# A recurrence of a transformer block: the offset, bonus and gate of a round's outputs move from VectorE to GpSimd, and their copies stand one level later

## The reference, cut to what matters

```python
    _, y = lax.scan(step, s0, (tm(r4), tm(w4), tm(k4), tm(v4), tm(kk), tm(a4)))
    y = tm(y)
    mean = jnp.mean(y, axis=-1, keepdims=True)
    var = jnp.mean(jnp.square(y - mean), axis=-1, keepdims=True)
    yn = ((y - mean) * lax.rsqrt(var + RWKV_LN_EPS)).reshape(B, S, RWKV_WIDTH)
    yn = yn * lnx_w.astype(f32) + lnx_b.astype(f32)
    bonus = (jnp.sum(r4 * k4 * r_k.astype(f32), axis=-1, keepdims=True) * v4).reshape(B, S, RWKV_WIDTH)
    return ((yn + bonus) * g.astype(f32)).astype(p.dtype)
```

## Time and profile before

| | |
|---|---|
| median of 3 runs | 2664.47 us |
| span of the profiled execution | 2661.1 us |
| PE busy | 2627.1 us, 99% |
| DVE busy | 1938.4 us, 73% |
| ACT busy | 1381.1 us, 52% |
| POOL busy | 133.1 us, 5% |
| chain that ended last | PE 97%, DVE 2%, ACT 1% |
| recurrence and heads | about 290 to 458 us of the span |

### The profile page before, as it was taken

How to read it: one execution, slowest core, us unless ns; L and a number is a source line. 1 busy time by engine, 2 the same in 40 slices (tenths; PEclk the granted TensorE clock), 3 DMA queues, 4 the chain that set the end, 5 groups by cost and what they waited for, 6 DMA issues and landing times.

```text
span 2661.1 us, 46024 instructions
## 1 busy us (share of the span) xinstructions
PE 2627.1 (99%) x16912; PEld 2260.6 (85%) x16912; DVE 1938.4 (73%) x2963; ACT 1381.1 (52%) x2143; POOL 133.1 (5%) x146
## 2 busy tenths in 40 slices
PE   9999998999999999999999999999999999999998
PEld 8888887889888888888888888888888888888886
DVE  6677776777777877878887666578877656765675
ACT  5555565666544534535554454345455535553553
POOL 4500001301000000000000000000000000000000
PEclk9999999999999999999999999999999999999999
DMA  7555202565787888888778855677665565565554
GB/s 236 188 184 175 74 4 99 196 197 181 279 302 274 287 299 275 295 285 281 276 272 308 291 179 184 202 274 281 243 210 190 192 192 186 190 196 192 182 190 150
DMA packets 158927, 578.41 MB, mean 217 GB/s; under 512 B 18032, under 2 KB 18576, under 8 KB 157712
## 3 DMA queue, kind: packets, MB, share of 16 engines
q1 hardware_dynamic: 155792, 563.61, 62.4%
q10 hardware_dynamic: 1936, 9.44, 0.9%
q0 software_dynamic: 1008, 2.71, 0.4%
HBM read 572.81 MB, written 2.11 MB: 216 GB/s over the span
## 4 chain that ended last, share of the span: by engine, by line
PE 97%; DVE 2%; ACT 1%; issue 0%; DMA 0%; POOL 0%; DVEq 0%; ACTq 0%
PE ps L2623 35%; PE ps L2627 18%; PE ps L2702 12%; PE ps L2703 12%; PE ps L2704 12%; PE ps L1091 1%; PE ps L1737 1%; PE ps L1104 0%; PE ps L1115 0%; PE ps L1008 0%; PE ps L2686 0%; PE ps L2687 0%; PE ps L2685 0%; PE ps L2734 0%; PE ps L656 0%
## 5 line engine op out<-in xcount | busy, mean ns | idle before, releaser
L2194 DVE TENSOR_TENSOR wlo<-raw,whi 128x1024 fp32r<-128x1024 f32 x872 | 1058.9, 1230 | 523.1 <-ACT whi L1861 519.9
L1861 ACT ACTIVATE whi<-raw 128x1024 fp32r<-128x1024 f32 x872 | 904.5, 1056 | 794.7 <-PE ps L2627 387.3
L2623 PE MATMUL ps<-xn,whi 128*128 128x512 f32 x3760 | 940.9, 392 | 2.8 <-DVE xn L2273 1.4
L2623 PEld LDWEIGHTS ps<-xn,whi 128*128 128x128 f32 x3760 | 674.7, 188 | 123.3 <-issue 2.8
L2627 PEld LDWEIGHTS ps<-xn,wlo 128*128 128x128 f32 x3760 | 510.9, 191 | 37.4 <-DVE wlo L2194 0.4
L2627 PE MATMUL ps<-xn,wlo 128*128 128x256 f32 x3760 | 520.9, 282 | 0.0
L2702 PE MATMUL ps<-whi,act_in 128*128 128x512 f32 x1120 | 436.0, 389 | 0.0
L2704 PE MATMUL ps<-whi,act_in 128*128 128x512 f32 x1120 | 435.7, 389 | 0.0
L2703 PE MATMUL ps<-wlo,act_in 128*128 128x512 f32 x1120 | 435.7, 389 | 0.0
L2702 PEld LDWEIGHTS ps<-whi,act_in 128*128 128x128 f32 x1120 | 210.2, 188 | 44.6 <-DVE wlo L2194 1.0
L2704 PEld LDWEIGHTS ps<-whi,act_in 128*128 128x128 f32 x1120 | 210.2, 188 | 43.7
(11 more groups left out here) (346 smaller groups left out, 2228.7 us busy)
## 6 DMA issues: line engine op xcount, KB each, us to landing
raw<-in_stream SPq DMA_DIRECT2D x872, 512.0 KB, 4.3
adaw<-in_ada SPq DMA_DIRECT2D x96, 512.0 KB, 5.7
adaq<-in_ada SPq DMA_DIRECT2D x96, 512.0 KB, 5.3
memx<-in_memT ACTq DMA_DIRECT2D x1, 2048.0 KB, 10.7
gate_row<-gates POOLq DMA_DIRECT2D x2, 1024.0 KB, 7.5
h<-in_xT SPq DMA_DIRECT2D x3, 512.0 KB, 5.2
lwa<-in_lora ACTq DMA_DIRECT2D x2, 512.0 KB, 4.6
lwa<-in_lora ACTq DMA_DIRECT2D x1, 1024.0 KB, 6.3
```

Of the source, the lines that this page charges most:

```text
L1861: act.activation(whi[:, r, :], raw[:, r, :], ACT.Copy).then_inc(hi_done, 1)
L2194: dve.tensor_tensor(wlo[:, r, :], raw[:, r, :], whi[:, r, :].bitcast(F32), ALU.subtract)\
L2623: return pe.matmul(ps[:, lin.bank(g, t), :], whi[:, (p0 + s) % RING, c * 512 + t * P:c * 512 + (t + 1) * P], x[:, 2 * s + c, :], start=s + ...
```

## The change

GpSimd gets three steps under semaphores of its own (`tail_p`): `bl` adds the norm's offset to the bonus in place, as soon as VectorE has written the bonus (a round ahead); `yo` adds the sum to the normed outputs; and `yg` multiplies by the gate. VectorE keeps only `yn` of the three. GpSimd's new loop over the four rounds stands ahead of its loop over the eight heads. `high` now waits for GpSimd's `yg`. In rounds 1 to 3 it stands after the `c2` copies (in rounds 1 and 2 after the sigmoids too), and `low_part` after the work of level 2, right ahead of `doubled(i, 3)`. For round 3, `high(3)` stands after `turned_copy(1)` and `head(0)`, `low_part(3)` after the low part of head 0, and the load of `memx` two heads later.

```diff
-    YD = steps("tail_d", "yd yc ve vi yn yo yg lo")
+    YD = steps("tail_d", "yd yc ve vi yn lo")
+    YP = steps("tail_p", "bl yo yg")
...
+        for i in range(4):
+            for g in lanes:
+                q = 2 * (i % 2) + g
+                PD.wait(pool, g, i, "bo")
+                YP.done(pool.tensor_scalar(bo[q][:, :], bo[q][:, :], col("lnx_b", 2 * i + g), None, ALU.add), g, "bl")
+                YP.wait(pool, g, i, "bl")
+            for g in lanes:
+                q = 2 * (i % 2) + g
+                YD.wait(pool, g, i, "yn")
+                YP.done(pool.tensor_tensor(y1[g][:, :], y1[g][:, :], bo[q][:, :], ALU.add), g, "yo")
+                YP.wait(pool, g, i, "yo")
+                YP.done(pool.tensor_tensor(yq[g][:, :], y1[g][:, :], gg[q][:, :], ALU.mult), g, "yg")
         for k in range(8):
             HD.wait(pool, 0, 0, f"rc{k}")
...
         def high(i):
             for g in lanes:
                 for z in lanes:
-                    YD.wait(act, z, i, "yg")
+                    YP.wait(act, z, i, "yg")
...
-            if i:
-                high(i - 1)
             product(i, 2)
             if more:
                 sigmoids_a(act, i + 1)
+            if i:
+                high(i - 1)
+            if more:
                 gate_a(act, i + 1)
...
         turned_copy(0)
-        high(3)
         turned_copy(1)
         head(0)
-        for g in lanes:
-            act.wait_ge(YD.sems[g], RWKV_ALL)
-        act.dma_start(e["memx"][:, :, :], A["memT"]).then_inc(e["mem_in"], 16)
+        high(3)
         preload(act, ACT.Exp)
         for k in range(2, 9):
+            if k == 3:
+                for g in lanes:
+                    act.wait_ge(YD.sems[g], RWKV_ALL)
+                act.dma_start(e["memx"][:, :, :], A["memT"]).then_inc(e["mem_in"], 16)
...
-                yd_(i, g, "yn", dve.scalar_tensor_tensor(y, y, col("lnx_w", n), spread_bank(i, g), ALU.mult, ALU.mult), True)
-                yd_(i, g, "yo", dve.scalar_tensor_tensor(y, y, col("lnx_b", n), bo[q][:, :], ALU.add, ALU.add), True)
-                yd_(i, g, "yg", dve.tensor_tensor(yq[g][:, :], y, gg[q][:, :], ALU.mult))
+                yd_(i, g, "yn", dve.scalar_tensor_tensor(y, y, col("lnx_w", n), spread_bank(i, g), ALU.mult, ALU.mult))
...
             doubled(i, 1)
-            if i:
-                low_part(i - 1)
...
             else:
                 maxima(1)
+            if i:
+                low_part(i - 1)
             doubled(i, 3)
...
             normed(i)
-        low_part(3)
...
+            if k == 0:
+                low_part(3)
```

More of the change, by code:

```diff
@@ L877, in normed @@
             for g in lanes:
-                n, q = 2 * i + g, 2 * (i % 2) + g
-                y = y1[g][:, :]
+                n, y = 2 * i + g, y1[g][:, :]
                 YT.wait(dve, g, i, "vb")
-                yd_(i, g, "yn", dve.scalar_tensor_tensor(y, y, col("lnx_w", n), spread_bank(i, g), ALU.mult, ALU.mult), True)
-                yd_(i, g, "yo", dve.scalar_tensor_tensor(y, y, col("lnx_b", n), bo[q][:, :], ALU.add, ALU.add), True)
-                yd_(i, g, "yg", dve.tensor_tensor(yq[g][:, :], y, gg[q][:, :], ALU.mult))
+                yd_(i, g, "yn", dve.scalar_tensor_tensor(y, y, col("lnx_w", n), spread_bank(i, g), ALU.mult, ALU.mult))
         def low_part(i):
```

## The result

The median went from 2664.66 us (7 runs, 2662.23 to 2666.00) to 2670.82 us (7 runs, 2669.06 to 2676.67). The ratio is 1.0027, with a 95% interval of 1.0018 to 1.0036: slower by 6.2 us (0.23%), where 7.2 were predicted. The profiled execution of the changed kernel took 2670.74 with a span of 2668.9, so 1.8 around it.

A forecast was written before the change was run, and what follows sets the result against it. TensorE, busy 99% of the span, was taken as the bound, so only its waits count. 0.96 + 0.65 + 4.83 + 0.73 = 7.2 us takes the median from 2664.47 to 2671.7; 8-in-10 range 2667.5 to 2676.5.

The forecast's parts named there:

- GpSimd's queue: At the end, scaling of head 0 waits behind round 3's four moved operations, delaying TensorE's turning: +4.83 us, the main term.
- the sign that the prediction named: GpSimd's first scaling starts 5 to 7 us later against the end of `state` in round 3.
- Level 3: Low parts ahead of the level 3 merges delay these in rounds 1 and 2: 0.48 us each, +0.96 in all.
- `c3`: In round 3 the high parts behind `c2` push table load, exponentials and `c3` later on ScalarE: +0.65 us.
- Four steps leave VectorE: Relieving VectorE of about 2 us a round gains 0; bound on the gain 0.5 a round, 2 us in all.
- Rival 3: VectorE was the bound after all, at each round's end: faster, 4 us less, 2660.5; chance 0.06.
- `high(3)` and `memx`: On ScalarE at the end, `high(3)` ahead of the exponential's table +0.48, `memx` issue ahead of head 5's exponentials +0.25: +0.7 us.
- Rival 2: Queue partly absorbed at the end, heads 4 to 7 catching up 2 to 3 us: loss 4.5, time 2669.0; chance 0.17.
- Loads: First `mix_out` loads and `memx` at the end: `memx` lands 0.3 us ahead of ScalarE's second split; cost 0, up to +2.
- The clock: TensorE's clock falls again after the head turnings and recovers at the same point: 0; 1 to 4 us if only in `mix_out`.
- Rival 1: Slower by much more, through clock, late `memx` or GpSimd operations of 1.01: with 3 us more 2674.7; chance 0.17.
- The shared port: GpSimd beside VectorE costs 0.1 us per operation reading two SBUF inputs; as an exclusive lock, 0.4 in all.

The follow-up runs named there:

- after: The changed kernel itself, in its first profiled execution: 2670.74 us, where the changed kernel's median was 2670.82.
- again: The changed kernel once more, unchanged, a single execution for a second profile: 2668.83 us.
- queue: The changed kernel with GpSimd scaling heads 0 to 3 ahead of round 3's `yo` and `yg`: median 2.5 us under the changed kernel, 4.1 over the unchanged one.
- tail: The changed kernel with round 3 as before the change, rounds 0 to 2 as changed: median 5.4 us under the changed kernel, 1.2 over the unchanged one.
- late: The changed kernel with low parts behind level 3's next step and copies behind `c3`: median 0.9 us under the changed kernel, 5.9 over the unchanged one.
- place: The changed kernel with rounded copy and low part back at their old places in rounds 1 to 3: median 1.3 us under it, 5.3 over the unchanged kernel.
- before: The kernel without the change, in its profiled execution (span 2661.1 us) or its runs (median 2664.66 us beside the changed kernel).
- rounds: The kernel before the change with only `yo` and `yg` of rounds 0 to 2 moved to GpSimd, old places kept: 2664.91 against 2664.30 us, 1.0002.
- chain: The unchanged kernel with its end reordered and the last four `scores` in TensorE's round 3 gaps: 46.43 us from round 2's `yn` to `mix_out`, 47.28 unchanged.
- fill: The unchanged kernel with the last four `scores` put into TensorE's waits of round 3: median 1.6 us under it, the ratio's interval including 1.
- chain_only: The unchanged kernel with only its end reordered (both `yn` first; `high(3)`, `low_part(3)`, `memx` later), `scores` in a row: 2664.60 against 2664.46 us.

## Why the prediction was right

The steps in its order, with what the two profiles of the changed kernel measured:

```
term                                   predicted  after  again
start of round 0's yn                    0        -0.17  -0.50
level 3 merges, rounds 1 and 2          +0.96     +0.83  +1.02
c3 in round 3 (to yn of round 3)        +0.65     +2.26  +0.49
GpSimd's queue (yn to turning)          +4.83     +4.55  +4.54
high(3), memx (turning to mix_out)      +0.73     +0.52  +0.38
sum at mix_out                          +7.17     +7.99  +5.93
```

- **GpSimd's queue, the main term: right in mechanism, 0.28 too large.** queue and tail each remove it by another edit. The four operations take 0.72 to 0.73, and the price was 0.74; the error is mostly in the distance, 0.09 added to all four. An operation that needs the one ahead starts 0.08 after its end, an independent one before it (0.68 from start to start), so 2.99 to the scaling and not 3.32. Against the end of the state, the sign that the prediction named, the first scaling starts 5.7 later in again and 7.4 in after, outside of its 5 to 7 by the 1.67 of the clock.
- **The estimate of 0.56.** The estimate of 0.56 from the Trainium skill (GPSIMD Engine Reference, section 3.1) is refuted for this size: 0.72 to 0.73 in all rounds. With it the sum would have been 0.7 less, 6.5, which is nearer to the 6.4 measured, but by luck: the queue's term would have been 4.1 for a measured 4.55, and the terms that were too large elsewhere would have made up for it.
- **Level 3: right.** 0.47 a round, 0.94 for 0.96; late and place take it away. The table's +0.83 is against a round 1 of before that was itself 0.1 long, and its +1.02 has 0.2 of the pause in round 2.
- **`c3`: right, a little large.** 0.52 at TensorE's doubling for 0.65. Of the +2.26 in the row of the table 1.67 is the clock's. What the prediction didn't see is that the old place would have cost 0.2 too, with `yg` on GpSimd.
- **Four steps leave VectorE: nothing, right.** The rounds got longer, not shorter; rounds shows the move by itself at 1.0002, with no stretch shorter for it. Rival 3, faster because VectorE was the bound, is refuted.
- **`high(3)` and `memx`: half right.** `high(3)` cost 0.47 for 0.48. The issue of `memx` cost nothing where I had 0.25: it ran from 454.66 beside head 4's exponentials, and head 5's started 1.51 after head 4's with it.
- **Nothing absorbed.** Rival 2 wanted heads 4 to 7 to catch up 2 to 3 us. The shift is 7.98 at the table and 7.99 at `mix_out`. GpSimd's gap ahead of head 4 (2.99) is no slack, since what ends it is the reciprocal behind head 4's exponentials, which are as late.
- **Loads: the 0 was right, the slack wrong.** The prediction had `memx` issued 1.5 behind the start of head 4's exponentials, which left 11.0 us to its use and a slack of 0.3. It was issued 0.07 behind that start (454.66 for 454.59), which left 12.2 us and a slack of 1.7. In place and queue the load took 12.0 and 12.5 to land, and only in queue was it late, by 0.3.
- **The clock: 0 for the cause, not for the execution.** The fall behind the two turnings came and went without a cost to the chain of heads in after, as argued; in chain a fall a little later on that chain cost 1.2, so this was partly luck. One that I had not looked for, at 435, took 1.67 in the profiled execution and nothing in again. Rival 1's size was partly there, for a reason outside the change.
- **Around the span.** I added 3.4, the distance of the profiled span from the median. It is 1.8 in every execution that has both (2668.9 and 2670.74 for the changed kernel, 2667.0 and 2668.83 in again). The other 1.6 was that the profiled execution of before was a quick one: by the same 1.8 an estimated 2662.9, against the median of 2664.47 that I had. So the hit at 2670.82 for 2671.7 is the sum of waits of about 6.4 (7.99 - 1.67 + 0.17 in after, 5.93 + 0.50 in again), over medians whose own difference is 6.2.
- **The shared port: as small as taken.** `bl` ran right behind `yg`, not late in the round:

```profile
378.04 0.72 POOL L336 TENSOR_TENSOR yq<-y,gg 128x256 f32<-128x256 f32 x1
378.74 1.94 POOL L329 TENSOR_SCALAR bo<-bo,par 128x256 f32<-128x256 f32 x2
```

The merges beside such stretches took 1.58 as against 1.57 in the earlier trace rows, and `yn` no more than before. But neither is an operation with two inputs in SBUF (the merges read a mask and PSUM), and in rounds 0 to 2 of the changed kernel none stands beside `bl`, so this says little about the port. In place, where the pair of `bl` of round 3 stands beside the low parts, it took 2.11 instead of 1.94, and the low parts their 0.76. The Trainium skill (SBUF — State Buffer, section on the two separate sides) has the loser blocked for the whole of the other's operation. While GpSimd scaled, `yo` and `yg` on VectorE looked like this in fill, and one `yo` in chain_only like the row below:

```profile
442.04 0.68 DVE L882 SCALAR_TENSOR_TENSOR y<-y,par,bo 128x256 f32<-128x256 f32 x1
442.75 0.65 DVE L883 TENSOR_TENSOR yq<-y,gg 128x256 f32<-128x256 f32 x1
```

```profile
441.58 0.76 DVE L893 SCALAR_TENSOR_TENSOR y<-y,par,bo 128x256 f32<-128x256 f32 x1
```

Instead of 0.42 to 0.48 that is up to 0.3 more, less than half of one scaling of GpSimd (0.60 for 128x128, 0.92 for 128x256). GpSimd pays as well, which the prediction left out. In chain_only the eight scalings took 6.40 instead of 5.95, and the two beside the low part 1.85 instead of 1.50:

```profile
437.77 6.40 POOL L328 TENSOR_SCALAR sm<-sm,sx__217 128x128 f32<-128x128 f32 x8 [179.49 <-DVE sx__217 L918]
445.92 1.85 POOL L328 TENSOR_SCALAR sm<-sm,sx__217 128x128 f32<-128x128 f32 x2 [1.75 <-DVE sx__217 L918]
```

A block for the whole of the other's operation is in none of the rows that I read, on either side.

## What to carry to other kernels

Before moving work to an idle engine, read its queue at the place where the moved steps will stand: it works in order, and steps that wait for a late input hold up everything behind them, here eight scalings that had long been ready (4.55 of 6.4 us). An engine that already waits right behind the steps which leave it gains nothing; its waits get longer by as much. Price a moved step also by what stands behind its new place: one step in front of the merges cost 0.47 a round, one place further on nothing. And before a difference of half a microsecond in one profile is explained, see whether a stretch that no edit touched scatters as much; the places were shown by one number of round 1 that repeats to the hundredth in twelve profiles.

## What the runs showed of the hardware that was not expected

- **TensorE's clock falls at other places in each execution of the same program.** The granted clock was below 1 in 440 to 452 in before, in 432 to 440 and 444 to 460 in after, in 440 to 456 in again, in 400 to 404 and 448 to 456 in tail, in 396 to 408 and 448 to 460 in chain, in 328 to 336 and 448 to 456 in fill (whose `yn` of round 0 is 1.5 late), nowhere from 300 to 500 in chain_only. Where it hits a stretch in which TensorE is full it costs 0.9 to 2.3 us (1.67 in after and late, about 0.9 in tail, about 2.3 in chain's round 2), as much as any effect of a place here. So a profile is read by stretches, and the stretch with the fall is compared with another execution before a cause is named. The Trainium skill (TensorE: Matmul & The Clock Gate, Part 1) tells of such differences from run to run at a kernel's start; here they are in the middle too.
- **GpSimd's distance between operations** depends on whether the next needs the last one's result: 0.80 to 0.81 from start to start if so, 0.68 if not, for operations of 0.72. From the start of `yn` on VectorE to GpSimd's `yo` it is 0.62, of which `yn` itself takes 0.48: a hand-over of 0.14.
- **The issue of a DMA by ScalarE** (0.36 for `memx`) had 0.15 of idle time behind it, ahead of the table load before, and none when it ran beside an exponential.
